# Second attention of a two-block transformer: rounded parts for values and probabilities, and the division by the softmax's total moved behind the turn

## The reference

```python
sc = einsum('bhqd,bhkd->bhqk', qi, k) * scale + ci[..., None] - c[:, :, None, :]   # FOX
sc = where(valid, einsum('bhqd,bhkd->bhqk', qi, kb) * scale + bias, NEG)          # CHK
p  = softmax(sc, axis=-1)
out = einsum('bhqk,bhkd->bhqd', p, v)            # for each block of 128 queries
...
merged = g_a * (o_a @ w_branch_a) + g_b * (o_b @ w_branch_b)
x = x + merged @ w_out
```

## Time and profile before

| | |
|---|---|
| median of 3 runs | 1928.05 us (1926.7 to 1928.11) |
| the profiled execution | 1927.73 us, its span 1925.9 us |
| PE busy | 1899.8 us, 99% of the span |
| DVE, ACT, POOL busy | 1009.0, 664.0, 998.5 us (52%, 34%, 52%) |
| granted TensorE clock | 0.998 of full speed |

### The profile page before, as it was taken

One profiled execution on the slowest core, in us unless ns is written; L12 is line 12 of the kernel. 1 busy time (PEld: TensorE's weight loads), 2 busy tenths in 40 slices (PEclk: granted clock), 3 DMA queues, 4 the chain that ended last, 5 costly groups with the idle time before them and its releaser, 6 DMA issues.

```text
span 1925.9 us, 26977 instructions
## 1 busy us (share of the span) xinstructions
PE 1899.8 (99%) x9708; PEld 1602.1 (83%) x9708; DVE 1009.0 (52%) x1863; ACT 664.0 (34%) x1260; POOL 998.5 (52%) x851
## 2 busy tenths in 40 slices
PE   8999999999999999999999999999999999999998
PEld 6788888888888988888878887888888888888886
DVE  6535663686555554454654457554444444444455
ACT  5135554546544453454521233331111111111134
POOL 4442237622222212112368884477777767777784
PEclk9999999999999999999999999999999999999999
DMA  4311113331111111102212213121211111211113
GB/s 138 110 44 29 33 39 104 83 124 42 42 42 51 28 40 50 43 19 67 77 50 55 55 28 132 54 66 44 75 50 52 44 44 45 76 55 44 55 33 131
DMA packets 148379, 115.26 MB, mean 60 GB/s; under 512 B 11528, under 2 KB 140048, under 8 KB 148256
## 3 DMA queue, kind: packets, MB, share of 16 engines
q1 hardware_dynamic: 135456, 93.34, 16.3%
q10 hardware_dynamic: 12800, 20.28, 3.2%
HBM read 105.15 MB, written 11.59 MB: 61 GB/s over the span
## 4 chain that ended last, share of the span: by engine, by line
PE 93%; DVE 3%; issue 1%; POOL 1%; ACT 1%; DMA 1%; SPq 0%; POOLq 0%; DVEq 0%; ACTq 0%
PE ps L1189 7%; PE ps L1063 6%; PE ps L1064 6%; PE ps L1065 6%; PE ps L1523 5%; PE ps L1522 5%; PE ps L1524 5%; PE ps L1485 5%; PE ps L1483 5%; PE ps L1484 5%; PE ps L1178 4%; PE ps L1046 3%; PE ps L1047 3%; PE ps L1048 3%; PE ps L1111 2%; PE ps L1112 2%
## 5 line engine op out<-in xcount | busy, mean ns | idle before, releaser
L821 POOL TENSOR_TENSOR w_hi<-raw,ones 128x512 fp32r<-128x512 f32 x100 | 112.7, 1127 | 636.2 <-PE ps L1065 484.2
L2936 DVE TENSOR_TENSOR X<-ps,X 128x1024 f32<-128x1024 f32 x112 | 137.2, 1225 | 204.7 <-PE ps L1524 204.7
L2127 ACT ACTIVATE ps<-ps 128x512 f32<-128x512 f32 x64 | 37.3, 582 | 510.9 <-DVE ps L2913 510.8
L1063 PE MATMUL ps<-h_hi,w_hi 128*128 128x512 f32 x480 | 191.7, 399 | 0.0
L1064 PE MATMUL ps<-h_lo,w_hi 128*128 128x512 f32 x480 | 188.1, 392 | 0.0
L1065 PE MATMUL ps<-h_hi,w_lo 128*128 128x512 f32 x480 | 187.8, 391 | 0.0
L1522 PE MATMUL ps<-hid_hi,slot_hi 128*128 128x512 f32 x448 | 174.3, 389 | 0.0
L1523 PE MATMUL ps<-hid_lo,slot_hi 128*128 128x512 f32 x448 | 174.3, 389 | 0.0
L1524 PE MATMUL ps<-hid_hi,slot_lo 128*128 128x512 f32 x448 | 174.3, 389 | 0.0
L969 POOL TENSOR_TENSOR slot_hi<-up,ones 128x512 fp32r<-128x512 f32 x88 | 91.7, 1042 | 114.5 <-PE ps L1524 112.0
L1189 PEld LDWEIGHTS ps<-v_seq,probs_t 128*128 128x128 f32 x1056 | 137.1, 191 | 11.9 <-issue 1.8
(11 more groups left out here) (453 smaller groups left out, 4931.8 us busy)
## 6 DMA issues: line engine op xcount, KB each, us to landing
raw<-in_w_in SPq DMA_DIRECT2D x88, 256.0 KB, 2.8
down_raw<-in_w_down SPq DMA_DIRECT2D x72, 256.0 KB, 2.8
up<-in_w_up SPq DMA_DIRECT2D x32, 512.0 KB, 4.1
raw<-in_w_out SPq DMA_DIRECT2D x32, 256.0 KB, 2.7
gate_ring<-in_w_in SPq DMA_DIRECT2D x24, 256.0 KB, 3.3
x_in<-in_x SPq DMA_DIRECT2D x8, 512.0 KB, 8.0
raw_b<-in_w_out SPq DMA_DIRECT2D x16, 256.0 KB, 2.7
x_store<-X ACTq DMA_DIRECT2D x8, 512.0 KB, 2.6
```

Of the source, the lines that this page charges most:

```text
L1063: pe.matmul(o, w1, h_hi[:, k, c], start=k == 0, stop=False)
L2936: dve.tensor_tensor(X[:, q], pair(q % 2), X[:, q], ALU.add).then_inc(x_added, 1)
```

## The change

It touches the 8 rounds of the second attention only.

- The values are held in two parts, side by side: for each key block and head 128 columns, 64 of the rounded values and 64 of the rest (`v_st`). ACT rounds (`round_v`, n = 0), DVE makes the rest (`rest_v`, n = 1).
- In `weigh_split` the values are the held operand and the probabilities move: 256 columns of float32r for a key block, 128 rounded and 128 of the rest. The result comes out turned, one half of the partitions for each part of the values, so the sum of the parts has to be made across partitions: `copy_low` on ACT, `add_low` and `add_high` on DVE.
- ACT writes the rounded probabilities (`probs_hi`), and DVE now makes the rest (`probs_lo`), into a ring of 3 groups where there were 4. `turned_copied` comes from DVE now.
- `scale` goes. DVE makes the reciprocal over 64 columns (`inverse`), PE turns it (`turn_inverse`, in the place of `turn_heads`), and `finish` multiplies, in the place of `store`.
- On PE, `turn(n - 1)` now stands ahead of `weigh_split(n - 2)`.
- Some buffers lie elsewhere (`v_st0`, `x_top[1]`), two small semaphores are shared, and SP's first loads of the branch weights wait for the end of round 6.

```diff
+                def weigh_split(n):                      # PE
+                    qb, hh, groups, g = units[n]
+                    pe.wait_ge(o_scaled, 1 + u0 + max(n - 1, 0))
+                    if hh == 1:
+                        pe.wait_ge(heads_stored, 1 + pair_no * NB + qb)
+                    for gi, (kb, cnt) in enumerate(groups):
+                        pe.wait_ge(turned_copied, 1 + group0 + (g + gi + 1))
+                        for b in range(cnt):
+                            mm = pe.matmul(bank(2 + hh, 2 * P),
+                                           buf["v"][st][:, kb + b, hh].rearrange("p a d -> p (a d)"),
+                                           probs_ring[(g + gi) % 3][:, b].rearrange("p a n -> p (a n)"), ...)
+                        mm.then_inc(pv_done, 1)
...
+                def probs_hi(n):                         # ACT
+                    _, _, groups, g = UNITS[kind][n]
+                    for gi, (_, cnt) in enumerate(groups):
+                        act.wait_ge(turned, 1 + group0 + (g + gi + 1))
+                        act.wait_ge(pv_done, 1 + group0 + max(g + gi - 2, 0))
+                        act.activation(probs_ring[(g + gi) % 3][:, 0:cnt, 0],
+                                       bank(6 + (g + gi) % 2, cnt * P)..., ACT.Copy).then_inc(p_hi_made, 1)
+
+                def copy_low(n):
+                    qb, hh, groups, g = UNITS[kind][n]
+                    act.wait_ge(pv_done, 1 + group0 + (g + len(groups)))
+                    if hh == 1:
+                        act.wait_ge(heads_turned, 1 + pair_no * NB + (qb + 1))
+                    act.wait_ge(o_scaled, 1 + u0 + max(n - 1, 0))
+                    act.activation(o_seq[0:HD, n % 2], ps[HD:P, 2 + hh, 0:P], ACT.Copy).then_inc(low_copied, 1)
...
                     events(n)
-                    if 1 <= n <= 16:
+                    if kind != SWA:
+                        if 1 <= n <= 16:
+                            probs_hi(n - 1)
+                        if 2 <= n <= 17:
+                            copy_low(n - 2)
...
+                if kind != SWA:                          # DVE
+                    for n in range(16 + 2):
+                        if n < 16:
+                            mask(n)
+                        if 1 <= n <= 16:
+                            inverse(n - 1)
+                        if n >= 4 and n % 2 == 0:
+                            finish((n - 4) // 2)
+                        events(n)
+                        if n >= 2:
+                            add_low(n - 2)
+                        if 1 <= n <= 16:
+                            probs_lo(n - 1)
+                        if n >= 2:
+                            add_high(n - 2)
+                    finish(NB - 1)
+                    return
```

More of the change, by code:

```diff
@@ L545, in build @@
         x1_stored = sem("x1_stored")
-        x1_loaded = [sem(f"x1_loaded{k}") for k in range(KT)]
         f_scaled = sem("f_scaled")
@@ L699, in load_a @@
                 sp.dma_start(raw[:, 0], wa_v[:, :, i * P:(i + 1) * P]).then_inc(a_raw_loaded, 16)
+            sp.wait_ge(pv_done, 1 + GROUP0[FOX] + (PAIRS - 1) * GROUPS[FOX])
             load_branch(0)
@@ L1180, in turn @@
                         mm.then_inc(turned, 1)
+                def weigh_split(n):
[8 more added lines that the diff above has]
+                                           buf["v"][st][:, kb + b, hh].rearrange("p a d -> p (a d)"),
+                                           probs_ring[(g + gi) % 3][:, b].rearrange("p a n -> p (a n)"),
+                                           start=(gi == 0 and b == 0),
+                                           stop=(gi == len(groups) - 1 and b == cnt - 1))
+                        mm.then_inc(pv_done, 1)
                 def weigh(n):
@@ L1205, in attention @@
                         tail()
-                    if n >= 2:
+                    if n >= 2 and kind == SWA:
                         weigh(n - 2)
@@ L1209, in attention @@
                         turn_v(g_v, pair_no, group0)
-                    if n == 0 and pair_no not in (0, PAIRS):
+                    if n == 0 and kind == SWA and pair_no:
                         turn_heads(pair_no - 1, NB - 1)
@@ L1215, in attention @@
                         turn(n - 1)
-                    if n >= 4 and n % 2 == 0:
+                    if n >= 2 and kind != SWA:
+                        weigh_split(n - 2)
+                        if n % 2:
+                            turn_inverse(pair_no, (n - 3) // 2)
+                    if n >= 4 and n % 2 == 0 and kind == SWA:
                         turn_heads(pair_no, (n - 4) // 2)
@@ L2357, in scale, with inverse, add_low @@
                                       inv_total[:, s:s + 1], None, ALU.mult).then_inc(o_scaled, 1)
+                def inverse(n):
+                    qb, hh, _, _ = units[n]
+                    dve.wait_ge(probs_ready, u0 + n + 1)
+                    dve.reciprocal(inv_rows[:, qb % 2, hh * HD:(hh + 1) * HD],
+                                   total[:, n % 4:n % 4 + 1].broadcast_to([P, HD])).then_inc(inverted, 1)
+                def add_low(n):
+                    qb, hh, _, _ = units[n]
+                    dve.wait_ge(low_copied, u0 - 16 * PAIRS + n + 1)
+                    low = o_seq[0:HD, n % 2]
+                    mine.done(dve.tensor_tensor(low, ps[0:HD, 2 + hh, P:2 * P], low, ALU.add))
@@ new lines, in probs_lo @@
+                def probs_lo(n):
+                    _, _, groups, g = units[n]
+                    for gi, (_, cnt) in enumerate(groups):
+                        slot = probs_ring[(g + gi) % 3]
+                        dve.wait_ge(p_hi_made, group0 - GROUP0[CHK] + (g + gi + 1))
+                        dve.tensor_tensor(slot[:, 0:cnt, 1],
+                                          bank(6 + (g + gi) % 2, cnt * P).rearrange("p (b n) -> p b n", n=P),
+                                          f32(slot[:, 0:cnt, 0]), ALU.subtract).then_inc(turned_copied, 1)
@@ new lines, in add_high, with finish @@
+                def add_high(n):
+                    qb, hh, _, _ = units[n]
+                    mine.wait()
+                    if hh == 0:
+                        dve.wait_ge(heads_stored, 1 + pair_no * NB + max(qb - 1, 0))
+                    dve.tensor_tensor(o_sum[hh * HD:(hh + 1) * HD, qb % 2], ps[0:HD, 2 + hh, 0:P],
+                                      o_seq[0:HD, n % 2], ALU.add).then_inc(o_scaled, 1)
+                def finish(qb):
+                    dve.wait_ge(heads_turned, 1 + pair_no * NB + (qb + 1))
+                    dve.wait_ge(o_scaled, 1 + u0 + 2 * qb + 2)
+                    dve.tensor_tensor(O[:, pair_no % (2 * PAIRS), qb * P:(qb + 1) * P], ps[:, 3, 2 * P:3 * P],
+                                      o_sum[:, qb % 2], ALU.mult).then_inc(heads_stored, 1)
@@ L2364, in attention @@
                         scale(n - 2)
-                    if n == 1 and pair_no not in (0, PAIRS):
+                    if n == 1 and pair_no:
                         store(pair_no - 1, NB - 1)
@@ L2665, in events @@
                 def events(n):
+                    if n == 1:
+                        rest_v(r)
                     if r == 2 * PAIRS - 1:
```

57 lines of the change are left out of this document (38 added, 19 removed).

## The result

The changed kernel takes 2028.53 us (median of 4 runs, 2026.06 to 2030.21) against 1927.61 us (4 runs, 1926.7 to 1928.11): 1.0523 of the time before, 95% interval 1.0505 to 1.0541, so 101 us slower. The forecast was 2001 us, with 1955 to 2045 as its range: the sign and the cause came as forecast; the loss is 28 us larger.

A forecast was written before the change was run, and what follows sets the result against it. The prediction took a closed loop of waits between DVE and ACT to replace PE as the bound in the eight rounds. Losses by round plus single work summed to 73 us: 1928 + 73 = 2001 us, range 1955 to 2045.

The forecast's parts named there:

- the ring: Closed loop of waits between DVE and ACT, from one mask to the next, predicted to outlast PE's step.
- The length of the ring: Sum of the loop's links for a 5-block unit: 4.07 us, against PE's step of 3.69 before and 3.2 after.
- A rounding: ACT's rounding for the next round, between exponential and probs_hi: 1.08 us more per step, six in each of rounds 0 to 6.
- The start that is held back: DVE instruction writing to another partition quarter waits for all before it: 0.08 us a unit, some 9 us, giving 2010.
- The sum by rounds: Added loss per round: 11.5 us in round 0, 8 in rounds 1 to 3, 7.1 in 4 to 6, 6 in 7.
- the lag: Deduction because copies and rests belong to the unit before, with fewer blocks: 1.0 us of the ring in rounds 1 to 3.
- entering the ring: Cost at a round's start, where the steps change from PE's to the ring's: 1.1 us in rounds 1 to 3.
- The round's end: Eight fill steps on PE (5.5 us) that wait for no ring, covering 3.2 us of its last pass.
- single work of ACT and DVE: One-off work within the ring: 5.7 us in round 1, 3.6 in round 7, 1.5 for a scan in round 2.
- The product: PE's product with the values: 0.12 us a block instead of 0.21, saving 47 us over 528 blocks.
- the rival at 1881 us: PE stays the bound and the kernel gets faster, needing a ring under 3.2 us at 5 blocks; 8 in 100.
- a fall for good: Rival: PE's clock drops to 1.2 of 2.4 GHz because of its waits, above 2200 us; 3 in 100.

The follow-up runs named there:

- e3: Changed kernel, with ACT's copies for the two units before (probs_hi, copy_low) moved ahead of the current unit's exponential: 1913.23 us, 0.9922 of the kernel before.
- e1: Changed kernel, with ACT's events(n) (roundings, logarithm, sigmoid) moved behind probs_hi and copy_low: 1982.27 us, 1.0281 of the kernel before.
- e2: Changed kernel, with DVE's probs_lo(n - 1) moved ahead of add_low(n - 2): 1989.54 us, 1.0321 of the kernel before.
- e8: Changed kernel, with PE's weigh_split(n - 2) put back ahead of turn(n - 1): 2029.76 us, 1.0524 of the kernel before.
- e4: Changed kernel, with a second, unused 64-column reciprocal on DVE in each of the 128 units: 2040.62 us, 1.0582 of the kernel before.
- e7: Changed kernel, with ACT's copies ahead of the exponential, probs_lo ahead of add_low, and a one-column reciprocal on DVE spread by ACT: 1904.00 us, 0.9874 of the kernel before.

## Why the prediction came out as it did

**PE isn't the bound any more; the ring is: right, and shown.** The order of calls alone, at equal work, moves the time by 115 us (e3), by 46 (e1) and by 39 (e2), while PE's order moves nothing (e8) and 64 us more work for DVE only 12 (e4). PE's idle time is put down to DVE's `probs_lo` as forecast, but it is 101.5 us, under the 110 to 130 that were named. Another part of the loss stands in PE's busy time: in the eight rounds it is 494.6 us here and 455.3 in e7, for as many instructions (2690 and 2689). Some 11 of these 39 us are the lower clock (an estimate from the granted clock of 0.95 to 0.98 in five of the rounds); no view takes the others apart. So idle time alone understates what PE lost.

**The length of the ring: right.** 4.07 us was summed, 4.11 and 4.32 in turn were measured. Link by link: mask 0.86 (0.87), exponential 0.95 (0.94), copies 0.79 (0.77), `copy_low` and the hand-over 0.31 (0.25), the two additions 0.41 (0.40), rest 0.79 (0.84). A rounding adds its 1.08: 5.19 us and 5.40 between such masks; the prediction had 5.1.

**The start that is held back: right in kind, a little short.** Every second step is longer by 0.21 us. In the timeline above, `add_high` at 483.78 starts while the rest (from 482.99, 0.87 long) is still under way, and the mask 0.20 after it; in the next step `add_high` writes to the other half of the partitions, starts at 487.98, when the rest (from 487.08) has ended at 487.95, and the mask starts 0.32 after it. That is the rule of the Trainium skill (VectorE: DVE Perf Modes, Two Vector instructions with no wait between them) which the prediction weighed at 0.08 a unit. The trace agrees with it, and makes it 0.11 a unit, some 12 us in 110 units. Left out of the sum, it is the largest piece of the 28 us that the rows let me name.

**The sum by rounds: the step that was mis-sized.** The timeline of DVE's masks in round 3, units 1, 4 and 15:

```profile
655.35 0.29 DVE L2400 CUSTOM_DVE_ANT_0 probs<-ps,bias_chk 128x128 f32<-128x128 f32 x1 [2.35 <-PE ps L1176]
...
666.44 0.56 DVE L2400 CUSTOM_DVE_ANT_0 probs<-ps,bias_chk 128x384 f32<-128x384 f32 x1
...
713.97 0.81 DVE L2400 CUSTOM_DVE_ANT_0 probs<-ps,bias_chk 128x640 f32<-128x640 f32 x1
```

and of the kernel before, the same units:

```profile
611.22 0.29 DVE L2345 CUSTOM_DVE_ANT_0 probs<-ps,bias_chk 128x128 f32<-128x128 f32 x1 [3.26 <-PE ps L1164]
...
621.57 0.55 DVE L2345 CUSTOM_DVE_ANT_0 probs<-ps,bias_chk 128x384 f32<-128x384 f32 x1
...
657.03 0.82 DVE L2345 CUSTOM_DVE_ANT_0 probs<-ps,bias_chk 128x640 f32<-128x640 f32 x1 [0.76 <-PE ps L1164]
```

From unit 4 to 15 the ring takes 47.5 us and PE took 35.5: +12.1. The prediction's own figures for these 11 steps are its 50.7 and 39.9 less a last step of 5.15 and 3.69, so 45.5 and 36.2: +9.3. Of the 2.0 that the ring is longer, 1.2 are the held starts (11 steps of 0.11). The other 0.8 lie in the steps of 3 and 4 blocks: up to the mask of unit 8, at 681.74, the ring takes 15.3 us, where the prediction's figures make 14.1 (2 x 2.9, 2 x 3.4, two roundings, less 0.7 for the lag), and 0.4 of that are held starts again. The 0.7 on the other side is that PE's old steps were a little shorter than reckoned.

The round's start came as forecast. From unit 1 to 4 the masks are 11.09 us apart against 10.35, but PE is busy for all of it, and from the scores of unit 1 to those of unit 4 it needs 9.74 us now and 9.73 before. What grew is how far each mask lies behind its scores, since ACT's copy and DVE's rest of the unit before now come in between: 0.7 us, where the prediction gave 1.1 for entering the ring and took 0.2 off for two cheaper blocks.

The round's end was the other term that failed. From the last mask to the next copy of the values the kernel after takes 14.1 us against 15.2: -1.1, where the prediction's terms make -2.6 (3.2 covered, 0.9 for ten cheaper blocks, +1.5 for the last step). PE is busy throughout there, but the granted clock is 0.88. In round 2, at 1.00, the same stretch takes 13.7 us (-1.6), and PE waits for 1.0 of it.

By rounds: forecast 11.5, 13.7, 9.5, 8, three times 7.1, 9.6 (with the terms for single work of ACT and DVE in their rounds); measured 16.3, 15.7, 12.4, 11.6, 9.9, 10.0, 10.0, 12.9. The shortfall is 2 to 5 us in each round, and no one round holds it. One term was too large and made up for a little of it: round 1 grew by 4.1 us more than round 3, where 5.7 had been put for the logarithm and the two exponentials.

**The product: cheaper, but by less than said.** 0.136 us a block instead of 0.12, so 0.074 saved and not 0.09: 39 us over 528 blocks, which e7's 40.6 us of PE's busy time bears out. In the changed kernel this didn't show at all, since the ring hid it; the rival at 1881 us ("PE stays the bound") is what e3 to e7 set up, and by these runs it lies at 1904, not at 1881: 8 us since the product is dearer, and 14 of waits, most of them in rounds 0 and 7, which have few fills, and some in 1 and 2. In round 7 of e7 PE waits for exponentials (2.8 us, its weight loads 4.3), DVE for ACT (12.7) and ACT for PE (13.4); no run took them apart, and what binds those rounds stays open.

**What was ruled out.** SP's new wait and the waits on `heads_stored`: no view names them among the waits of the rounds. The ring of 3 groups shows only as ACT's wait for a product ahead of `probs_hi`, 1.9 us in four times. PE's waits for DVE's rests and masks (74.6, 13.8 and 7.1 us) make up 95.5 of its 101.5. The clock did fall a little (0.98 in the rounds); see below.

## What to carry to other kernels

When work moves to engines with idle time, write down who waits for whom within one step before adding up busy shares: idle time that was a wait for the bound is slack only as long as the moved work doesn't tie the two idle engines to each other. On an engine that runs in order, put what concerns earlier units ahead of the instruction that waits for the current unit, unless something needs the current one sooner; here that alone was worth 115 us. And price a ring at each of its step sizes and where it ends, not only at its commonest step: here that one step was right to 0.04 us (to 0.25 where a start is held back), and the sum was still 3 us a round short.

## What the runs showed of the hardware

**After one wait of 2.01 us PE ran at the lower clock for some 3 us.** In the kernel before the granted clock was 1.00 in every round. In e3 PE has one wait of 2.01 us in round 2, behind a scan on DVE. PE's timeline there:

```profile
587.75 1.24 PE L1190 MATMUL ps<-ident,probs 128*128 128x128 f32 x5 [2.01 <-DVE probs_ring L2431]
588.64 1.42 PE L1202 MATMUL ps<-probs_ring,v_st 128*128 128x256 f32 x5
...
591.42 0.39 PE L1071 MATMUL ps<-h_lo,w_hi 128*128 128x512 f32 x1
```

and the stretches of 5 us around it, with the granted clock third from the end:

```profile
580.00:585.00 5.00, 4.99 (x30) 4.20 (x29) 4.75 (x16) 3.16 (x9) 0.00 (x0) 1.00 0.01 2
585.00:590.00 5.00, 2.99 (x16) 2.55 (x14) 4.74 (x10) 0.66 (x2) 2.44 (x2) 0.78 0.05 6
590.00:595.00 5.00, 5.00 (x30) 4.57 (x29) 3.34 (x10) 3.02 (x8) 0.00 (x0) 0.88 0.21 52
```

Five turns take 0.89 us from start to start instead of 0.46, five products about 1.2 instead of 0.68: for about 3 us TensorE ran at 1.2 GHz instead of 2.4, and then at full speed again with no further wait. The prediction had this as a fall for good, at above 2200 us.

The length of a wait doesn't tell by itself. In the changed kernel the clock fell behind a wait of 1.89 us at the end of round 3, and stayed up behind one of 1.99 us in round 4 (a matmul of 512 columns takes 0.63 us in the one case and 0.40 in the other):

```profile
713.79 0.74 PE L1190 MATMUL ps<-ident,probs 128*128 128x128 f32 x5 [1.89 <-DVE probs_ring L2431]
...
715.81 0.63 PE L1071 MATMUL ps<-h_lo,w_hi 128*128 128x512 f32 x1
...
790.27 1.06 PE L1190 MATMUL ps<-ident,probs 128*128 128x128 f32 x8 [1.99 <-DVE probs_ring L2431]
...
792.35 0.40 PE L1071 MATMUL ps<-h_lo,w_hi 128*128 128x512 f32 x1
```

Over a round such stretches lower the mean to 0.95 in rounds 0 and 7, to 0.98 in rounds 1 to 3, and not at all in rounds 4 to 6 (1.00). They are mostly hidden beside the ring: masks with a rounding stand 5.40 and 5.19 us apart in the part of round 0 that had 0.93, and 5.40 and 5.20 in that of round 3 that had 1.00. Where PE is the bound, at the end of round 3, they cost some 0.5 us against round 2 (14.1 and 13.7 us).

**A run of products of 256 columns, each with its own weights, took 0.136 us a block.** The product of the same width that the prediction went by, the second of the scores, is followed by the next matmul 0.12 us later. It has the held operand of the product ahead of it (`q_st`), while in the run of five the held operand changes each time. Whether that makes the difference no run shows.
